# Gathering the second block's expert inputs from float32 rows instead of three bfloat16 parts

## The reference, cut to what matters

```python
def _hier_moe(x, w_grp, b_grp, w_exp, b_exp, w_gate, w_up, w_down):
    ...
    eid = (g_idx[:, None] * EXPERTS_PER_GROUP + top_e).reshape(-1).astype(jnp.int32)
    ...
    def expert_block(args):
        idx, e = args
        xb = x_pad[idx]
        hdn = jax.nn.silu(xb @ w_gate[e]) * (xb @ w_up[e])
        return hdn @ w_down[e]

def second_block(x, ...):
    for i in range(DEPTH_2):
        mix = ...
        x = _layer_norm(ALPHA * x + mix, ln1_g[i], ln1_b[i])
        ffn = _hier_moe(x, moe_w_grp[i], moe_b_grp[i], moe_w_exp[i], moe_b_exp[i], moe_w_gate[i], moe_w_up[i], moe_w_down[i])
        x = _layer_norm(ALPHA * x + ffn, ln2_g[i], ln2_b[i])
```

## Time and profile before

| | us |
|---|---|
| runs before (3), median | 3821.57 |
| lowest, highest | 3815.26, 3823.08 |
| profiled execution, first to last instruction (span) | 3815.9 |
| TensorE matmuls busy | 2847.0 (75% of the span) |
| TensorE weight loads busy | 1552.1 (41%) |
| VectorE, ScalarE, GpSimd busy | 948.5, 630.3, 194.1 |
| layer 0: split_rows from, to | 1984.9, 2002.1 |
| layer 0: token_stage, first to last matmul | 2005.8 to 2495.4 |
| layer 1: split_rows from, to | 3248.4, 3265.9 |
| layer 1: token_stage, first to last matmul | 3269.9 to 3759.0 |

### The profile page before, as it was taken

The page is one execution under the profiler, slowest core; times in us unless marked ns, Lnnn a source line. Parts: engine busy times, 40 slices in busy tenths (PEclk is TensorE's granted clock), DMA queues, the critical chain, the costliest instruction groups (busy, mean ns, idle before and its releaser), DMA issues. The chain is left out here.

```text
span 3815.9 us, 41899 instructions
## 1 busy us (share of the span) xinstructions
PE 2847.0 (75%) x15777; PEld 1552.1 (41%) x15778; DVE 948.5 (25%) x1750; ACT 630.3 (17%) x1087; POOL 194.1 (5%) x174
## 2 busy tenths in 40 slices
PE   7997888264999996986539899833677575688893
PEld 4645888232333333443214444411323552344441
DVE  3602555313121213045240000000214352200002
ACT  3312221012101002023021111100213121211111
POOL 0003433000000000000000000000000000000000
PEclk9998999686999998997769999966888787899996
DMA  6141000250999983200017999933320001699995
GB/s 245 54 169 54 1 1 1 64 204 31 428 413 405 417 355 142 80 33 24 25 38 327 429 429 429 429 139 149 131 94 7 20 1 37 243 429 429 428 429 211
DMA packets 112775, 760.49 MB, mean 199 GB/s; under 512 B 21268, under 2 KB 26112, under 8 KB 72848
## 3 DMA queue, kind: packets, MB, share of 16 engines
q1 hardware_dynamic: 107760, 741.07, 47.7%
q0 software_dynamic: 3168, 14.68, 1.0%
q10 hardware_dynamic: 1728, 3.15, 0.2%
HBM read 728.71 MB, written 30.16 MB: 199 GB/s over the span
## 5 line engine op out<-in xcount | busy, mean ns | idle before, releaser
L1835 PE MATMUL bank<-ring,expert_in 128*64 128x512 f32 x2048 | 464.6, 608 | 55.4 <-DMA ring<-in_moe_w_up_dram 53.0
L1835 PEld LDWEIGHTS bank<-ring,expert_in 128*64 128x64 f32 x2048 | 161.1, 140 | 352.3 <-issue 349.6
L1846 PE MATMUL bank<-ring,hidden_T 128*64 128x512 f32 x1024 | 226.8, 595 | 41.3 <-ACT hidden_T L1798 41.3
L1621 PE MATMUL bank<-ring,expert_in 128*64 128x512 f32 x1024 | 224.7, 596 | 7.8 <-DVE expert_sum L1513 5.5
L1824 PE MATMUL bank<-onehot,x_part 128*128 128x128 bf16 x3072 | 180.9, 221 | 54.0 <-DVE onehot L1766 54.0
L1775 DVE TENSOR_TENSOR hidden<-silu_gate,bank 128x512 f32<-128x512 f32 x32 | 33.7, 1054 | 753.5 <-PE bank L1835 753.5
L233 PE MATMUL bank<-x_cols,ring 128*128 128x512 f32 (+2 forms) x480 | 208.2, 593 | 2.9 <-PEq L189 2.9
L1824 PEld LDWEIGHTS bank<-onehot,x_part 128*128 128x128 bf16 x3072 | 175.4, 99 | 78.6 <-DVE onehot L1766 54.3
L1846 PEld LDWEIGHTS bank<-ring,hidden_T 128*64 128x64 f32 x1024 | 71.7, 137 | 175.8 <-issue 149.5
L1621 PEld LDWEIGHTS bank<-ring,expert_in 128*64 128x64 f32 x1024 | 73.6, 138 | 156.8 <-issue 141.7
L233 PEld LDWEIGHTS bank<-x_cols,ring 128*128 128x128 f32 (+2 forms) x480 | 86.5, 181 | 122.0 <-issue 122.0
(11 more groups left out here) (547 smaller groups left out, 3569.3 us busy)
## 6 DMA issues: line engine op xcount, KB each, us to landing
ring<-in_moe_w_gate_dram SPq DMA_DIRECT2D x64, 2048.0 KB, 17.9
ring<-in_moe_w_up_dram SPq DMA_DIRECT2D x64, 2048.0 KB, 18.5
ring<-in_moe_w_down_dram SPq DMA_DIRECT2D x64, 2048.0 KB, 13.9
ring<-in_w_gate_dram SPq DMA_DIRECT2D x32, 2048.0 KB, 13.2
ring<-in_w_up_dram SPq DMA_DIRECT2D x32, 2048.0 KB, 14.5
ring<-in_w_down_dram SPq DMA_DIRECT2D x32, 2048.0 KB, 16.1
ring<-in_w_mod_dram SPq DMA_DIRECT2D x12, 2048.0 KB, 13.1
expert_rows<-expert_out SPq DMA_DIRECT2D x32, 512.0 KB, 18.6
```

Of the source, the lines that this page charges most:

```text
L1621: mm = pe.matmul(B[2 + 2 * part + b][rows, :], xe[:, dc, rows], ws[e][:, c, b * COLS:(b + 1) * COLS], start=(dc == 0), stop=(dc == NC - 1))
L1835: mm = pe.matmul(B[2 + 2 * part][rows, :], xe[:, c, rows], ws[e][:, c, :], start=(c == 0), stop=(c == NC - 1))
L1846: mm = pe.matmul(B[6 + b][rows, :], hT[:, c, rows], ws[e][:, c, b * COLS:(b + 1) * COLS], start=(c == 0), stop=(c == NF - 1))
```

## The change

The three parts and `split_rows` go from the second block (the first block's experts keep them). The gather reads X itself: chunk c of a tile is a view with a step of 8 floats (32 bytes) between columns, and the one-hot matrix is float32. For each chunk and tile there is one call instead of three: 32 calls in place of 96. `extra_slots` is changed in the same way. What is computed stays the same.

```diff
+def chunk_of(X, t, c):
+
+    return X[:, t, :].rearrange("p (q c) -> p c q", c=NC)[:, c, :]
+
 def token_stage(m, w, E, first_load, src, pos, out_rows):
...
-        oh = sb("onehot", [P, NT, 2, SLOTS], BF16)
+        oh = sb("onehot", [P, NT, 2, SLOTS])
...
                     for c in range(NC):
-                        k = 0
-                        for part in range(3):
-                            for t in range(NT):
-                                mm = pe.matmul(B[c // 4][:, c % 4 * P:(c % 4 + 1) * P], src[part][:, t, c * P:(c + 1) * P],
-                                               oh[:, t, :, :], start=(k == 0), stop=(k == 3 * NT - 1))
-                                k += 1
+                        for t in range(NT):
+                            mm = pe.matmul(B[c // 4][:, c % 4 * P:(c % 4 + 1) * P], chunk_of(src, t, c), oh[:, t, :, :],
+                                           start=(t == 0), stop=(t == NT - 1))
                     mm.then_inc(gathered, 1)
...
-        oh = sb("x_onehot", [P, NT, SLOTS], BF16)
+        oh = sb("x_onehot", [P, NT, SLOTS])
...
             for c in range(NC):
-                for part in range(3):
-                    for t in range(NT):
-                        mm = pe.matmul(B[0][:, c * SLOTS:(c + 1) * SLOTS], src[part][:, t, c * P:(c + 1) * P], oh[:, t, :],
-                                       start=(part == 0 and t == 0), stop=(part == 2 and t == NT - 1))
+                for t in range(NT):
+                    mm = pe.matmul(B[0][:, c * SLOTS:(c + 1) * SLOTS], chunk_of(src, t, c), oh[:, t, :],
+                                   start=(t == 0), stop=(t == NT - 1))
...
-        with ExitStack() as inner:
-            sbi = m.buffers(inner)
-            parts = [sbi(f"x_part{j}", [P, NT, D], BF16) for j in range(3)]
-            split_rows(m, X, parts, m.moe2[i] + RING)
-            token_stage(m, w, E, m.moe2[i], parts, pos, S["rows"])
-            extra_slots(m, w, E, parts, pos, count, S["rows"])
+        token_stage(m, w, E, m.moe2[i], X, pos, S["rows"])
+        extra_slots(m, w, E, X, pos, count, S["rows"])
```

## The result

| | median us | lowest, highest | runs |
|---|---|---|---|
| before | 3822.32 | 3815.26, 3823.08 | 4 |
| changed | 4054.81 | 4050.89, 4055.94 | 4 |

The changed kernel takes 1.0615 times as long (95% interval 1.06 to 1.063). Its profiled execution has a span of 4052.9 us, 237.0 more than that of before.

A forecast was written before the change was run, and what follows sets the result against it. The weight stream was taken to bound the kernel, TensorE after the change. Layers +100.2 and +100.6 and laps +9.7 give +210 on 3815.9, so 4026; 5.7 for the runs' median makes 4032 us, 8-in-10 range 3785 to 4090.

The forecast's parts named there:

- The forecast case: Token-stage gathers at 235 ns a record make TensorE the bound; 4032 us, own range 3980 to 4080, chance 0.55.
- The bound: Token-stage pair loop: the weight stream binds at 30.56 us a pair, TensorE ahead by 2.5 us; gather growth beyond is paid.
- The price of the step: Gather's weight loads: 235 ns a record, between 118 and 241, making a gather 15.0 us and a pair 37.7.
- The split stage: Stage before the second block's token stages: nothing hides it, so removing it saves 17.3 and 17.5 us, -34.8 in all.
- The first gathers: Gather opening each layer's token stage, alone on the path: 15.0 us against 7.72 and 7.14, +7.3 and +7.9.
- A: Rival for the gather: the step costs TensorE nothing, 118 ns a record, the split's gain is won; 3797 us, chance 0.25.
- The last pair: Last pair of each layer's loop: no longer waits for its up matrix, -2.3 us a layer.
- The laps: Three laps' gathers: 15.0 us each, +10.3, partly covered by waits for the up matrix; +9.7 us in all.
- Rival B: Pair loop: the clock falls during gathers, slowing transposes and half of down by 3.3 us a pair; 4131 us, chance 0.11.
- C: Rival for the gather: the step costs twice as much again, 460 ns a record; 4536 us, chance 0.05.
- D: Rival for the gather: a small surcharge, 132 to 150 ns a record; some 3810 to about 3855 us, chance 0.04.

The follow-up runs named there:

- step1: Changed kernel with adjacent columns in the gather's stationary operand, so channels no longer match the gate and up rows; 3795.48 us, 0.9934 of before.
- two_of_eight: Changed kernel with the 32-byte step in only two of the eight chunks and adjacent columns in the other six; 3846.11 us, 1.0063 of before.
- split_kept: Changed kernel with the split stage put back, its three parts written but not used; 4091.21 us.

## Why the prediction was right

4032 us was forecast and 4055 measured, +210 against +237 on the profiled executions. The forecast case came true; step by step:

- *The bound.* That the weight stream leads by 2.5 us a pair was the pivot. In step1 (gather +1.9 us) the weight stream still sets the pace, two_of_eight (gather +3.9) loses, and the change (gather +10.05) loses all beyond the margin. The share of the DMA engines was forecast to fall to 0.8, and is 0.83.
- *The price of the step.* 235 ns a record were forecast from ScalarE's and VectorE's copies, 241 measured. The upper of the two bounds, ScalarE's surcharge per element, was the right one. The argument behind it, a limit on the memory's side that is the same for every engine, fits two more rows: the record with 16 bytes in the moving operand is 1.80 ns a column, and a gather with the step takes the same time at the half clock (15.49 us at 0.50, 15.42 at 1.00). No row shows the limit itself, and it is not general: a bfloat16 load with 16 bytes pays 50 ns where a float32 load pays 137. The fixed time of some 0.2 us that the forecast takes off the copies is near what the kernel before has for very short instructions: 0.206 us for ScalarE on 4 columns (L2356), 0.175 for VectorE on 16 (L2323). The 6 ns come to 30 x 0.38 = 11 us.
- *The split stage.* -34.8 us forecast. In layer 1, from the end of the routing to the first gather, 3375.94 - 3371.22 = 4.7 us are left of 22.5 before (3247.46 to 3269.92), so -17.7; split_kept shows 35.1 for both layers in TensorE's waits and 36.4 in the time.
- *The first gathers.* 16.74 us from start to the first gate in layer 1 against 8.32 before, +8.4 where +7.9 was forecast. That the clock has not yet risen there, as A says, is seen in layer 0 before: 0.50 from 2005.78 to 2009.00 us, 0.84 from there to 2013.50.
- *The last pair.* -2.3 us forecast for the wait; from its gate to the end of down it went from 27.8 to 23.5 us, -4.2, since without the wait its up block does not take 8.78 us as in the earlier trace rows any more.
- *The laps.* +9.7 us forecast. Between the end of the last pair and the end of the last lap lie 163.2 us against 150.7, +12.5, of which some 3 are down blocks with a lower clock (14.1 us busy against 11.0; granted clock 0.68 and 0.72 in the first two laps, 1.00 in both before). A lap's gather takes 15.49 us, 15.0 forecast, but not for the reason in the sum: with adjacent columns it takes 13.91 (step1), so the half clock makes most of it and the step 1.6 us. That this term came out was luck.
- *The clock.* This is the term that the sum lacked. Rival B had it as a fall in every pair, 99 us; its 3.3 us a pair, with the transposes and half of down at the half clock, was the author's estimate, and no run shows it. What the changed kernel shows is nine pairs of 32 with 1.7 us more in down, at a granted clock of 0.81: 242.0 - 226.8 = 15 us. In its gather at 2054.66 the clock is 1.00. The case split was too sharp, forecast and B held together in part. With the 11 us of the step that makes 26, the miss of 27 to within the smaller terms. Such dips are not new, only their price is. In the kernel before eight of the 32 up blocks take 8.7 to 8.8 us instead of 7.09 (granted clock 0.81 to 0.82; 1.00 in the second row below), each right behind 2.2 to 2.3 us of waiting for its matrix, and the next wait is shorter:

```profile
2415.91 8.78 PE L1835 MATMUL bank<-ring,expert_in 128*64 128x512 f32 x32 [2.32 <-DMA ring<-in_moe_w_up_dram]
...
2446.49 7.09 PE L1835 MATMUL bank<-ring,expert_in 128*64 128x512 f32 x32 [0.63 <-DMA ring<-in_moe_w_up_dram]
```

  While the weight stream was the bound it took the 1.7 us up; with TensorE as the bound each dip is paid in full.
- *The rivals.* A is refuted by the change. Its total is met by step1, 3797 forecast and 3795 measured with the step gone, but in part by offsets: the laps, put at nothing, cost 6.9 us (157.6 against 150.7) since their gathers take 13.91 us at the half clock, and the last pairs, not counted, gave back 3.4 us each. C's 460 ns a record and 29 us a gather did not come: 241 ns and 15.42 us. D's break-even of 138 ns was not tried by itself; two_of_eight, 145 ns on average, lost 24 us.

## What to carry to other kernels

In these runs a float32 operand in SBUF whose columns stand 16 bytes apart cost TensorE 1.8 ns a column, on either side of a matmul (235 ns a record of 128 columns on the stationary side, 230 on the moving one), and with 32 bytes (tried for the stationary side, 241 ns) 1.9; ScalarE and VectorE needed about the same for an element with 32 bytes, 2.03 and 2.00 us for 1024. On the stationary side 8 bytes were nearly free at the full clock, 119 ns against 113. Before a split or a copy is removed, ask what else it did: here its value was the reordering that came with it, and a float32 copy in the right order beside the routing keeps that for some 2 us a layer instead of the split's 17. And read how far the second resource lies behind the bound: with 2.5 us of 30.6 in hand, a gather could grow by 1.9 us, as in step1, and not by 10.

## What the runs showed of the hardware that was not expected

- The price is a stair and not a slope: 113, 119, 235 and 241 ns a record for 4, 8, 16 and 32 bytes.
- A bfloat16 weight load with a step of 16 bytes pays only 50 ns (98 to 148), and 7 of them show in a record (56 to 63): the gather went from 5.37 to 6.03 us, and the kernel took 3813 us.
- Loads with the step take the same time at both clock levels (medians of 336 ns in the pairs at the full clock, 335 in the laps at 0.50); with adjacent columns, in step1, they went from 192 to 333 ns at the half clock. There a record takes 217 ns without the step and 242 with it.
- VectorE's copy of 16 elements took 1.87 us beside a GpSimd copy of X, and 0.17 without one.
- Gate and up loads in pieces of 2 KB instead of 16 KB lowered the stream from 429 to 402 GB/s.
- The granted clock dips at some down blocks (to 0.81 over the block in the changed kernel), 8.78 instead of 7.09 us: 9 of 32 in the changed kernel, more with the gather moved away (257.3 against 242.0 us busy), fewer with a step of 16 bytes (230.2), none in step1. In the kernel before it dips at up blocks behind 2.3 us of waiting instead (0.81 to 0.82), where the stream hides it. Its cause stays open.
